# Up projection of an MLP with stationary weights and moving tokens in a two-layer decoder kernel

## The reference

```python
h2 = rms_norm(x, norm2_g[l])
x = x + jnp.square(jax.nn.relu(h2 @ w_up[l])) @ w_down[l]

def rms_norm(x, g):
    y = x * lax.rsqrt(jnp.mean(x * x, axis=-1, keepdims=True) + EPS)
    return y * g
```

## Time and profile before

| | |
|---|---|
| three runs | 2988.55 us median (2987.88 to 2988.84) |
| profiled execution, span | 2989.6 us |
| its own time beside the span | none is given for this execution |
| PE busy | 2917.6 us, 98%, 13120 matmuls |
| PEld busy | 2389.9 us, 80% |
| DVE busy | 1748.7 us, 58% |
| ACT busy | 1355.1 us, 45% |
| POOL busy | 318.0 us, 11% |
| DMA | 558.65 MB, mean 187 GB/s |

### The profile page before, as it was taken

The page is one execution under the profiler, slowest core; times in us unless marked ns, Lnnn a source line. Parts: engine busy times, 40 slices in busy tenths (PEclk is TensorE's granted clock), DMA queues, the critical chain, the costliest instruction groups (busy, mean ns, idle before and its releaser), DMA issues.

```text
span 2989.6 us, 38386 instructions
## 1 busy us (share of the span) xinstructions
PE 2917.6 (98%) x13120; PEld 2389.9 (80%) x13120; DVE 1748.7 (58%) x1849; ACT 1355.1 (45%) x1673; POOL 318.0 (11%) x329
## 2 busy tenths in 40 slices
PE   7998899999999999999999989999999999999998
PEld 6776788888888888888877767888888888888887
DVE  4689655556555555555545896555565545555554
ACT  5443654444443444434445436444444434344443
POOL 1158300000000000000020682000000000000000
PEclk9999999999999999999999999999999999999999
DMA  7544456565655656555564444666556565565653
GB/s 270 187 162 131 151 170 210 192 228 197 203 185 191 191 188 188 189 188 190 186 220 169 149 141 145 183 208 225 197 200 202 188 190 190 186 192 185 196 184 127
DMA packets 274090, 558.65 MB, mean 187 GB/s; under 512 B 13168, under 2 KB 13168, under 8 KB 271376
## 3 DMA queue, kind: packets, MB, share of 16 engines
q1 hardware_dynamic: 266384, 523.53, 53.1%
q0 software_dynamic: 5888, 30.02, 3.4%
q10 hardware_dynamic: 1664, 3.15, 0.3%
HBM read 550.37 MB, written 6.29 MB: 186 GB/s over the span
## 4 chain that ended last, share of the span: by engine, by line
PE 88%; DVE 6%; issue 4%; ACT 1%; DMA 1%; DVEq 0%; POOL 0%; ACTq 0%; POOLq 0%
PE acc L545 28%; PE acc L547 28%; PE acc L546 28%; DVE conv_acc L1136 3%; PE tp L558 3%; PE sc L601 1%; DVE lo L1075 1%; ACT hi L805 1%; PE tp L617 1%; DMA conv_bias<-in_conv_o_b 1%; DVE index L1154 0%; DVE index L1218 0%; DMA pos_i<-in_positions 0%; DVE head_sum L1257 0%; DVE s_buf L1166 0%
## 5 line engine op out<-in xcount | busy, mean ns | idle before, releaser
L1075 DVE TENSOR_TENSOR lo<-raw,hi 128x1024 fp32r<-128x1024 f32 (+1 forms) x1008 | 1237.6, 1230 | 1191.9 <-ACT hi L805 1182.9
L805 ACT ACTIVATE hi<-raw 128x1024 fp32r<-128x1024 f32 (+1 forms) x1008 | 1055.7, 1048 | 1489.4 <-PE acc L547 1485.3
L545 PE MATMUL acc<-hi,hT_hi 128*128 128x512 f32 x2304 | 924.7, 401 | 34.5 <-DVE lo L1075 34.4
L547 PE MATMUL acc<-hi,hT_lo 128*128 128x512 f32 x2304 | 903.6, 392 | 0.0
L546 PE MATMUL acc<-lo,hT_hi 128*128 128x512 f32 x2304 | 902.9, 392 | 0.0
L545 PE MATMUL acc<-hi,bT_hi 128*128 128x512 f32 x1408 | 556.4, 395 | 0.0
L547 PE MATMUL acc<-hi,bT_lo 128*128 128x512 f32 x1408 | 548.8, 390 | 0.0
L546 PE MATMUL acc<-lo,bT_hi 128*128 128x512 f32 x1408 | 548.5, 390 | 0.0
L545 PEld LDWEIGHTS acc<-hi,hT_hi 128*128 128x128 f32 x2304 | 436.0, 189 | 133.2 <-DVE lo L1075 44.6
L547 PEld LDWEIGHTS acc<-hi,hT_lo 128*128 128x128 f32 x2304 | 435.6, 189 | 93.9
L546 PEld LDWEIGHTS acc<-lo,hT_hi 128*128 128x128 f32 x2304 | 436.7, 190 | 87.0
(11 more groups left out here) (223 smaller groups left out, 1689.1 us busy)
## 6 DMA issues: line engine op xcount, KB each, us to landing
raw<-in_w_in SPq DMA_DIRECT2D x160, 1024.0 KB, 5.0
raw<-in_w_up SPq DMA_DIRECT2D x128, 1024.0 KB, 5.2
raw<-in_w_down SPq DMA_DIRECT2D x128, 1024.0 KB, 5.1
raw<-in_w_out SPq DMA_DIRECT2D x32, 1024.0 KB, 5.1
raw<-in_w_mem_kv SPq DMA_DIRECT2D x16, 1024.0 KB, 5.1
raw<-in_w_attn_o SPq DMA_DIRECT2D x16, 1024.0 KB, 5.1
raw<-in_w_conv_o SPq DMA_DIRECT2D x8, 1024.0 KB, 5.1
raw<-in_w_mem_o SPq DMA_DIRECT2D x8, 1024.0 KB, 5.1
```

Source lines behind the costliest of these rows:

```text
L545: pe.matmul(o, a1, w1, start=first and dk == 0, stop=False)
L547: mm = pe.matmul(o, a2, w1, start=False, stop=last and dk == 1)
L805: act.activation(hi[:, u % 4, :, 0:w], raw[:, c, 2 * (u % 2):2 * (u % 2) + 2, 0:w], ACT.Copy).then_inc(hi_ready, 1)
L1075: dve.tensor_tensor(lo[:, u % 4, :, 0:w], raw[:, u // 2, 2 * (u % 2):2 * (u % 2) + 2, 0:w], hi[:, u % 4, :, 0:w].bitcast(F32), ALU.subtrac ...
```

## The change

The up projection gets a function of its own, `up_unit`. A unit's weights are now the stationary operand, in four pieces f of 128 columns, and the 256 tokens are the moving one. The result has the hidden columns on the partitions and the tokens along the free axis (`accT`, a view of the same PSUM banks), which is how the down projection wants it. So the transposes of `hidden`, their waits and both semaphores' counts go. With tokens no longer on the partitions, `rstd` isn't applied at the Relu; `inv_mean = 1 / (mean + EPS)` is applied per token when the down projection's block is added to `x`. The two steps from PSUM for each token tile become one over 1024 columns. GpSimd's root for this norm goes; VectorE makes the reciprocal.

The core of the diff:

```diff
+            def up_unit(u, pair, first, last):
+                if first:
+                    pe.wait_ge(acc_free[pair], here.next(f"acc{pair}"))
+                pe.wait_ge(lo_ready, here.next("unit") + 8)
+                for dk in range(2):
+                    kt = 2 * u + dk
+                    for f in range(COL // P):
+                        o = accT[:, pair, f]
+                        fs = slice(f * P, (f + 1) * P)
+                        w1, w2 = hi[:, u % 4, dk, fs], lo[:, u % 4, dk, fs]
+                        pe.matmul(o, w1, hT_hi[:, kt], start=first and dk == 0 and f % 2 == 0, stop=False,
+                                  skip_group_check=True)
+                        pe.matmul(o, w1, hT_lo[:, kt], start=False, stop=False, skip_group_check=True)
+                        mm = pe.matmul(o, w2, hT_hi[:, kt], start=False, stop=last and dk == 1 and f % 2 == 1,
+                                       skip_group_check=True)
+                mm.then_inc(unit_done, 1)
...
                     if g < CB:
-                        unit(u, hT_hi, hT_lo, (2 * u, 2 * u + 1), COL, pair, u == 0, u == UNITS - 1)
+                        up_unit(u, pair, u == 0, u == UNITS - 1)
                     else:
                         if m == 32:
-                            emptied(("hidden", 2, 1))
+                            pe.wait_ge(hid_low, here.next("hid_low", CB - 1))
                         if m == 38:
-                            emptied(("hidden", 3, 1))
+                            pe.wait_ge(hid_low, here.next("hid_low"))
                         unit(u, bT_hi, bT_lo, (2 * u, 2 * u + 1), COL, pair, u == 0, u == UNITS - 1)
-                    b, t = divmod(m - 11, UNITS)
-                    if b in range(CB) and t in range(T):
-                        if t == 0:
-                            pe.wait_ge(hid_ready, here.next("hid_ready"))
-                        fill(("hidden", b, t), [hidden[:, b % 2, t, k * P:(k + 1) * P] for k in range(4)])
...
                     b, r = divmod(m - 12, UNITS)
                     if r == 0 and b in range(CB):
-                        if first and b == 0:
-                            act.wait_ge(rstd_ready, here.next("rstd_ready"))
+                        pair = (1, 0)[b % 2]
                         block_done(b * UNITS + 7)
-                        for t in range(T):
-                            ins = act.activation(hidden[:, b % 2, t], acc[:, (1, 0)[b % 2], t], ACT.Relu,
-                                                 scale=rstd[:, 2, t:t + 1])
-                        ins.then_inc(hid_relu, 1)
+                        act.activation(hidden[:, b % 2], accT[:, pair], ACT.Relu).then_inc(hid_relu, 1)
...
-                    b, t = divmod(m - 15, UNITS)
-                    if b in range(CB) and t in range(T):
-                        take_high(("hidden", b, t), bT_hi[:, 4 * b:4 * b + 4, t * P:(t + 1) * P])
+                    b, r = divmod(m - 14, UNITS)
+                    if r == 0 and b in range(CB):
+                        act.wait_ge(hid_sq, here.next("hid_sq"))
+                        act.activation(bT_hi[:, 4 * b:4 * b + 4, :], hidden[:, b % 2], ACT.Copy
+                                       ).then_inc(hid_high, 1)
...
-            def add_block(b, pair, e):
+            def add_block(b, pair, e, scaled_by=None):
...
-                dve.tensor_tensor(xb, acc[:, pair], xb, ALU.add).then_inc(x_new, 1)
+                if scaled_by is None:
+                    ins = dve.tensor_tensor(xb, acc[:, pair], xb, ALU.add)
+                else:
+                    for t in range(T):
+                        ins = dve.scalar_tensor_tensor(xb[:, t], acc[:, pair, t], scaled_by[:, t:t + 1], xb[:, t],
+                                                       ALU.mult, ALU.add)
+                ins.then_inc(x_new, 1)
...
                     if first and m == X_MEAN:
-                        means(2, sq_sum)
+                        dve.wait_ge(squared, here.next("squared", T * CB))
+                        link(dve.tensor_reduce(mean_sq[:, 2], sq_sum[:, :, :], AX_X, ALU.add))
+                        link(dve.tensor_scalar(mean_sq[:, 2], mean_sq[:, 2], 1.0 / D, EPS, ALU.mult, ALU.add))
+                        link(dve.reciprocal(inv_mean[:, :], mean_sq[:, 2]))
...
-                    b, t = divmod(m - 15, UNITS)
-                    if b in range(CB) and t in range(T):
-                        here.next("fill")
-                        kts, cols = slice(4 * b, 4 * b + 4), slice(t * P, (t + 1) * P)
-                        take_low(("hidden", b, t), bT_lo[:, kts, cols], bT_hi[:, kts, cols])
+                    b, r = divmod(m - 15, UNITS)
+                    if r == 0 and b in range(CB):
+                        dve.wait_ge(hid_high, here.next("hid_high"))
+                        dve.tensor_tensor(bT_lo[:, 4 * b:4 * b + 4, :], hidden[:, b % 2],
+                                          bT_hi[:, 4 * b:4 * b + 4, :].bitcast(F32), ALU.subtract
+                                          ).then_inc(hid_low, 1)
```

More of the change, by code:

```diff
@@ L156 @@
 PER = {
-    "layer": {"group": GROUPS, "unit": GROUPS * UNITS, "acc0": 35, "acc1": 35, "fill": 112, "tp0": 56, "tp1": 56,
-              "tp_hi": 78, "score": 28, "sc0": 15, "sc1": 14, "squared": 24, "x_new": 20,
-              "dve_step": 153, "pool_step": 106, "gain_in": 48, "mem_in": 32, "front_in": 16 * FRONT_DMAS,
-              "ln_in": 32, "bias_in": 32 * CB, "parked": 32, "x_back": 16, "mean_ready": 3, "rstd_ready": 3,
+    "layer": {"group": GROUPS, "unit": GROUPS * UNITS, "acc0": 35, "acc1": 35, "fill": 80, "tp0": 40, "tp1": 40,
+              "tp_hi": 46, "score": 28, "sc0": 15, "sc1": 14, "squared": 24, "x_new": 20,
+              "dve_step": 155, "pool_step": 106, "gain_in": 48, "mem_in": 32, "front_in": 16 * FRONT_DMAS,
+              "ln_in": 32, "bias_in": 32 * CB, "parked": 32, "x_back": 16, "mean_ready": 2, "rstd_ready": 2,
               "scaled": 10, "ik_here": 2, "ikwT_here": 1, "ik_turned": 1, "iq_turned": 2,
@@ L167 @@
               "gate_in": 12, "gate_tanh": 12, "bias_used": CB, "merged_ready": CB,
-              "hid_relu": 16, "hid_ready": 16},
+              "hid_relu": 16, "hid_sq": 16, "hid_high": 16, "hid_low": 16},
     "merge": {"group": 4, "unit": 32, "acc0": 3, "acc1": 3, "fill": 2, "tp0": 1, "tp1": 1, "tp_hi": 2,
@@ L171 @@
               "merged_ready": 1},
-    "ffn": {"group": 8, "unit": 64, "acc0": 4, "acc1": 4, "fill": 8, "tp0": 4, "tp1": 4, "tp_hi": 8,
-            "x_new": 4, "hid_relu": 4, "hid_ready": 4},
+    "ffn": {"group": 8, "unit": 64, "acc0": 4, "acc1": 4,
+            "x_new": 4, "hid_relu": 4, "hid_sq": 4, "hid_high": 4, "hid_low": 4},
 }
@@ L294, in build @@
         index = at("index", [P, T, SEQ], S + 26 * kb)
-        hidden = at("hidden", [P, 2, T, COL], S + 22 * kb)
+        hidden = at("hidden", [P, 2, COL // P, SEQ], S + 22 * kb)
         glu_a = at("glu_a", [P, T, CONV], S + 30 * kb)
@@ L338, in build @@
         mean_sq = keep("mean_sq", [P, 3, T])
-        rstd = keep("rstd", [P, 3, T])
+        rstd = keep("rstd", [P, 2, T])
+        inv_mean = keep("inv_mean", [P, T])
         head_sum = keep("head_sum", [P, 8])
@@ L357, in build @@
         acc = ctx.enter_context(nc.psum_tensor("acc", [P, 2, T, COL], F32))
+        accT = acc[:, :, :, :].rearrange("p i t c -> p i (t c)").rearrange("p i (f s) -> p i f s", s=SEQ)
         tp = ctx.enter_context(nc.psum_tensor("tp", [P, 2, 4, P], F32))
@@ L430, in build @@
         hid_relu = sem("hid_relu")
-        hid_ready = sem("hid_ready")
+        hid_sq = sem("hid_sq")
+        hid_high = sem("hid_high")
+        hid_low = sem("hid_low")
         NAMES = ["group", "unit", "acc0", "acc1", "fill", "tp0", "tp1", "tp_hi", "score", "sc0", "sc1",
@@ L441, in build @@
                  "inv_ready", "probs", "gate_in", "gate_tanh", "bias_used", "merged_ready",
-                 "x_new", "ikwT_here", "hid_relu", "hid_ready"]
+                 "x_new", "ikwT_here", "hid_relu", "hid_sq", "hid_high", "hid_low"]
         chunked = {"p": P, "k": 4}
@@ L1353, in mlp @@
                     if m == 3:
-                        add_block(CB - 1, 0, -1)
+                        add_block(CB - 1, 0, -1, None if first else inv_mean)
                         if first:
@@ L1435, in _ @@
                 origin[0] = here.now("unit")
-                add_block(CB - 1, 0, -1)
-                here.next("rstd_ready", 2)
+                add_block(CB - 1, 0, -1, inv_mean)
+                here.next("rstd_ready")
         @block.gpsimd
@@ L1629, in _ @@
                 pool.dma_start(gain[:, :], rows(norm2_g[l])).then_inc(gain_in, 16)
-                root(2)
-                here.next("fill", T * CB + T * CB * FFN // D + T * (CB - 1))
+                here.next("fill", T * CB + T * (CB - 1))
                 pool.wait_ge(scaled, here.next("scaled", T + CB))
```

6 lines of the change are left out of this document (3 added, 3 removed).

## The result

The changed kernel takes 3003.44 us (median of 4 runs, 3001.38 to 3007.94) beside 2988.7 us (4 runs, 2987.88 to 2989.8) of the kernel before in the same comparison: a ratio of 1.0052, 95% interval 1.0039 to 1.0065. It is slower by half a per cent. The forecast was 2957.3, 1% faster, so the prediction was wrong in size and in sign. All times here are of executions with the clock nearly full (0.993 to 0.998 over the span); one execution of the kernel of experiment 6 had 0.798 from end to end, took 3417.96 us and is left out everywhere.

A forecast was written before the change was run, and what follows sets the result against it. The prediction took TensorE, by spacing of matmul starts, as the bound; -32.4 + 0.5 + 0.6 = -31.3 us from 2988.55 gave 2957.3 us, 1.05% less. Range 2954 to 2987 us, the forecast's own 2954 to 2967.

The forecast's parts named there:

- Steps 1 and 2: TensorE, MLP: removing 256 hidden transposes and the wait on the last transposed half saves 4.05 us a pass, -32.4 us.
- Steps 3 and 4: ScalarE/VectorE Relu, copies and subtractions merged to 1024 columns; GpSimd's root replaced by VectorE reciprocal: costed at nothing.
- Step 5: Up projection: a weight load per 256 columns, load hidden, matmuls 0.1133 us apart, units stay 2.72 us: change 0.
- Rival B: Up units: fixed share per matmul, 120.1 ns each, +41.8 us, 2999 us; chance 0.16 (B and beyond).
- Rival D: Up matmuls: weight loads run in series with no stream under them, 3633 us; chance 0.02.
- Rival A: Up matmuls: 128-column loads push spacing to 0.118 us, +28.2 us, 2985.5 us; chance 0.09.
- Rival C: MLP up blocks: removed time is hidden anyway; 2973 us if half the gain goes; chance 0.13 together with in-between values.
- Step 6: Down projection's add_block on VectorE: one 1218 ns addition becomes two scaled ones of 742 ns, 1.48 us, +0.27 each.
- the 0.27: Extra us of the scaled additions, exposed at the end of each layer: 2 x 0.27 = +0.5 us.
- six slips of 0.1: Last pass of each layer, three blocks each: later additions delay TensorE's transposes by 0.1 us each, +0.6 us.
- forecast +1.1: Cost of the scaled additions: +0.5 us at the layer ends and +0.6 us in the last passes.

The follow-up runs named there:

- experiment 6: Changed kernel with TensorE's two middle MLP passes of a layer written out instead of looped: 2996.6 us, measured again 2997.51 us.
- experiment 1: Changed kernel with the up projection's matmuls as before the change (tokens stationary, 512 weight columns moving): 2960.55 us, ratio 0.9904.
- Experiment 7: TensorE's two middle passes written out, in the kernel of experiment 1 (wide): 2955.5 us; in the kernel before: 2987.83 us.
- experiment 8: Changed kernel with one hi-weight load serving hT_hi and hT_lo as 512 moving columns, lo weights 256: 2986.87 us looped, 2981.2 us with middle passes written out.
- experiment 2: Kernel before with only the up projection's matmuls turned as in the change (weights stationary, 256 tokens moving), transposes kept: 3025.26 us, one run.

## Why the prediction was wrong, point by point

**Steps 1 and 2, transposes and the wait before unit 38: right.** -4.05 us a pass was forecast; experiment 1 shows 174.10 in the second pass, which is 178.13 less 4.03. Experiment 7 (wide, written out) is the forecast's own case, every step of the change but the shape of the up matmul: its MLP takes 1414.9 us, 32.1 less than before, and it runs in 2955.5 us, where the sum said 2957.3.

**Steps 3 and 4, merged steps and the root: right, nothing.** No idle time of TensorE in the MLP's up and down parts of those passes is left.

**Step 5, the spacing of 256-column matmuls: this is the step that failed**, and with it the sign. I took 0.1133 us from the earlier trace rows, since it was half of 0.2267 to a tenth of a nanosecond, and concluded that the stream costs by the column. That row differed from the up projection in two things, the moving columns (256, not 512) and the weight columns (80, not 128), and the two effects happened to cancel into a round half: 213.3 / 2 + 6.7 against (213.3 + 13.3) / 2. The right reading is one share for each matmul, and half of it for narrow weights. The term of the sum was 0 and measured 6144 x 6.67 ns = +41.0 us; the MLPs of the two written-out kernels, with narrow matmuls and with wide ones, differ by 1456.0 - 1414.9 = 41.1. Rival B had the mechanism, the place and the size (120.1 ns, +41.8, 2999 us), at a chance of 0.16. What it had wrong is its last part: the share isn't in proportion to the weight columns (64 and 112 pay the same). I weighed against it one coincidence of two numbers, where the row gave no way to tell the two effects apart. A prediction with such a row should have put B near even. The calculation beside it was sound but for one reading that changes nothing: from span 2989.6 and median 2988.55 it concludes that nothing lies around the span, and each run here takes 1.6 to 1.7 us more than its own span.

The rest of step 5 was right: the load is hidden. It has its own least time, about 111.6 ns for 128 columns, close to the 0.11 read from the earlier trace rows, and the 120 ns aren't set by it. Rival D, loads in series, would have been 223 ns. The rule of the Trainium skill from which D came ("TensorE: Matmul & The Clock Gate", "The mechanism") is contradicted by this trace: loads of 128 columns over all rows run beside a stream of 107 ns, and both together take 120. Rival A, the near miss at 118, didn't happen as such, but its pace came back in experiment 8. Rival C was refuted by experiment 1.

**Step 6, the scaled addition: right in size, but hardly felt.** Two additions of 742 ns, as the earlier trace rows gave. The slot with them, and the layer change, in VectorE's timeline and TensorE's:

```profile
898.98 1.40 DVE L1365 SCALAR_TENSOR_TENSOR x_tok<-acc,inv_mean,x_tok 128x512 f32<-128x512 f32 x2
900.61 1.23 DVE L1090 TENSOR_TENSOR lo<-raw,hi 128x1024 fp32r<-128x1024 f32 x1 [0.23 <-ACT hi L822]
...
1504.16 1.41 DVE L1365 SCALAR_TENSOR_TENSOR x_tok<-acc,inv_mean,x_tok 128x512 f32<-128x512 f32 x2 [8.45 <-PE acc L551]
...
1510.00 0.79 PE L549 MATMUL acc<-hi,hT_hi 128*128 128x512 f32 x1 [5.87 <-DVE lo L1090]
```

The two overlap by 0.08 and last 1.40 us, not 1.48; the next `lo` still waits 0.23 us for ScalarE (0.36 in the earlier trace rows; 0.1 forecast). At the layer change TensorE starts 5.84 us after the addition does, and 5.86 before, but 5.90, 6.09 and 6.11 in the profiles of experiments 7 (wide), 6 and 1, so whether the 0.27 is felt there can't be told. At the end of layer 2 it is felt: from the start of the last addition to the end of the span pass 8.27 us (2992.36 to 3000.63) against 8.10 before (2981.47 to 2989.57), +0.17. The six slips of 0.1 can't be found: the last pass of layer 1 grew by 1.06 us, like the second pass (1.09). Of the forecast +1.1, two or three tenths are there.

**What the prediction didn't have: the stall.** +8.5 us in the profile, 6 to 7 us in the medians (3003.44 against 2996.6 and 2997.5). No row of before could show it, since before has no fetch in that pass. But the change alters the code of TensorE's loop, and a rival that asks when these instructions come would have been possible. More instructions alone would not have been the right question, as experiments 1 and 2 show.

## What to carry to other kernels

A matmul with a new weight load pays a share of its own beside its columns; so before stationary and moving operand are exchanged, count the matmuls, not the columns, and put what the doubled number costs (here 3072 more matmuls at 13.33 ns, 41.0 us) against what the new layout saves (here 32.4 us). Take the price of a new shape from a row that differs in one size only; where it differs in two, a round ratio is no evidence, and the forecast should carry both readings. And after a change to the code of an engine's loop, longer or shorter, look for idle time by "issue" behind the loop's jump: writing two trips out gave 6 us back.

## What the runs showed of the hardware

- The share is seen only at the upper clock level. In the stalled stretch of the changed kernel, at 1.2 GHz, starts are 0.213 us apart, which is 256 / 1.2 = 213.3 with nothing added; behind the layer change, where the clock is at the same level, six 512-column matmuls take 2.56 us, 0.427 each, and 512 / 1.2 = 426.7:

```profile
1511.02 0.63 PE L551 MATMUL acc<-hi,hT_lo 128*128 128x512 f32 x1
...
1513.58 0.63 PE L551 MATMUL acc<-hi,hT_lo 128*128 128x512 f32 x1
```

  The Trainium skill ("TensorE: Matmul & The Clock Gate", section "Wait — 56ns, not 53.3ns?") says the same of the lower level, and gives 2.5 ns as the addition at the upper one; here it is 13.3 or 6.7. An estimate from its 2.5 ns puts the up matmuls 109.2 ns apart, where 120.0 was measured; that is also under the 111.6 found here for smaller ones.
- A matmul with a new 128-column load takes at least 111.6 ns (128 and 192 or 224 columns), so below about 236 moving columns, (111.6 - 13.3) x 2.4, narrower matmuls gain nothing. This is worked out from the table, between two sizes that were run.
- Alternating sizes cost more than the sum of their own paces (353.3 against 346.7 ns a pair), as transposes among matmuls do. Open.
- A pause of 2.8 us costs TensorE 4.3 us, since it starts again at the lower clock level (0.50 from 1142.70 to 1145.60).
- TensorE's code comes in packets of 16 KB, one for 255 to 257 of its instructions here. Behind a jump back it can stand still for it: 1.5 to 3.0 us, ending 1.3 to 1.5 us after a packet, in all twelve cases. Not every loop that fetches does so (experiment 2).
